# Three tiles in place of four in the row-wise opening of the gate projection of a transformer kernel

## The reference, cut to what matters

```python
for layer in range(DEPTH_2):
    ...
    h = h + rmsnorm(mix, gains[1])
    hn = rmsnorm(h, gains[2])
    ff = jnp.square(jax.nn.relu(hn @ w_up[layer])) @ w_down[layer]
    h = h + rmsnorm(ff, gains[3])
    gate = jax.nn.sigmoid(h @ w_ple_gate[layer])
    h = h + gate * (p[layer] @ w_ple[layer])
```

## Time and the profile before

| | us |
|---|---|
| median of 3 runs | 3325.06 (3324.88 to 3325.9) |
| the profiled execution, its own time | 3324.88 |
| its span | 3323.1 |
| PE busy | 3203.2 (96%) |
| POOL busy | 1743.3 (52%) |
| ACT busy | 1230.6 (37%) |
| DVE busy | 1214.4 (37%) |

### The profile page before, as it was taken

The page is one execution under the profiler, slowest core; times in us unless marked ns, Lnnn a source line. Parts: engine busy times, 40 slices in busy tenths (PEclk is TensorE's granted clock), DMA queues, the critical chain, the costliest instruction groups (busy, mean ns, idle before and its releaser), DMA issues.

```text
span 3323.1 us, 40114 instructions
## 1 busy us (share of the span) xinstructions
PE 3203.2 (96%) x15078; PEld 2612.8 (79%) x15078; DVE 1214.4 (37%) x2152; ACT 1230.6 (37%) x2217; POOL 1743.3 (52%) x1347
## 2 busy tenths in 40 slices
PE   8999999999999999999999898999999988999999
PEld 7888887777777787788888787877888776778887
DVE  4222322124555434223224655524111457341115
ACT  4332333333444435333224323234333345543333
POOL 6555655455554464465556213246555652475555
PEclk9999999999999999999999999999999999999999
DMA  4333222222222233333333102112333321223332
GB/s 163 98 92 101 86 86 76 83 82 77 64 61 61 70 106 97 88 98 98 98 96 95 54 26 58 39 54 80 101 96 95 96 70 39 64 85 100 96 101 86
DMA packets 149839, 275.58 MB, mean 83 GB/s; under 512 B 16528, under 2 KB 17808, under 8 KB 149520
## 3 DMA queue, kind: packets, MB, share of 16 engines
q1 hardware_dynamic: 149648, 273.02, 28.2%
HBM read 270.86 MB, written 2.10 MB: 82 GB/s over the span
## 4 chain that ended last, share of the span: by engine, by line
PE 85%; DVE 9%; POOL 3%; ACT 2%; issue 2%; DMA 0%; DVEq 0%; SPq 0%; ACTq 0%; POOLq 0%
PE PS L481 83%; PE PS L548 2%; POOL SM L2180 1%; DVE AR L1070 1%; POOL WL L2180 1%; DVE TMP L1070 1%; DVE ACC L1076 1%; DVE X L1070 1%; DVE AL L1070 1%; DVE HL L1076 1%; ACT AR L1795 1%; DVE SM L1070 1%; DVE TMP L1076 1%; DVE SM L1755 1%; DVE AR L1076 1%
## 5 line engine op out<-in xcount | busy, mean ns | idle before, releaser
L2180 POOL TENSOR_TENSOR WL<-RAW,WH 128x512 fp32r<-128x512 f32 x1002 | 1305.2, 1314 | 995.0 <-ACT WH L1795 994.2
L1795 ACT ACTIVATE WH<-RAW 128x512 fp32r<-128x512 f32 x1002 | 619.1, 627 | 1068.6 <-PE PS L481 1015.7
L481 PE MATMUL PS<-HH,WH 128*128 128x512 f32 x2296 | 914.0, 398 | 10.4 <-ACT WH L1795 7.1
L481 PE MATMUL PS<-HL,WH 128*128 128x512 f32 x2296 | 902.3, 393 | 7.9 <-DVE HL L1076 6.3
L481 PE MATMUL PS<-HH,WL 128*128 128x512 f32 x2296 | 901.5, 393 | 2.3 <-POOL WL L2180 2.3
L481 PE MATMUL PS<-AH,WH 128*128 128x512 f32 (+1 forms) x1504 | 584.3, 388 | 5.1 <-ACT AH L1795 3.5
L481 PE MATMUL PS<-AL,WH 128*128 128x512 f32 (+1 forms) x1504 | 582.1, 387 | 1.7 <-DVE AL L1070 1.1
L481 PE MATMUL PS<-AH,WL 128*128 128x512 f32 (+1 forms) x1504 | 580.9, 386 | 2.0 <-POOL WL L2180 2.0
L481 PEld LDWEIGHTS PS<-HL,WH 128*128 128x128 f32 x2296 | 435.7, 190 | 104.0 <-DVE HL L1076 12.1
L481 PEld LDWEIGHTS PS<-HH,WH 128*128 128x128 f32 x2296 | 435.3, 190 | 103.9 <-ACT WH L1795 7.4
L481 PEld LDWEIGHTS PS<-HH,WL 128*128 128x128 f32 x2296 | 434.8, 189 | 95.9 <-POOL WL L2180 4.2
(11 more groups left out here) (208 smaller groups left out, 2576.0 us busy)
## 6 DMA issues: line engine op xcount, KB each, us to landing
RAW<-in_wst SPq DMA_DIRECT2D x1002, 256.0 KB, 2.6
X<-in_x SPq DMA_DIRECT2D x8, 256.0 KB, 5.0
TMP<-in_p SPq DMA_DIRECT2D x8, 256.0 KB, 3.2
out<-X SPq DMA_DIRECT2D x8, 256.0 KB, 2.0
AR<-in_dm SPq DMA_DIRECT2D x1, 1024.0 KB, 5.3
AR<-in_mem SPq DMA_DIRECT2D x1, 1024.0 KB, 5.8
CST<-in_cst SPq DMA_DIRECT2D x1, 964.0 KB, 7.6
AR<-in_pos SPq DMA_DIRECT2D x2, 256.0 KB, 2.9
```

The costliest lines, as they stand in the source:

```text
L481: return e.matmul(o, l, r, start=a, stop=z, skip_group_check=True)
L1795: return e.activation(o, a, f, **kw)
L2180: return e.tensor_tensor(o, a, b, op)
```

## The change

The dictionary `opened`, which held the open PSUM banks by the kind of step, becomes two plain variables, `open_banks` and `mem_sum`, at all of its uses. In `e_open` the rows cover three output tiles in place of four; tile 3 is made by `lin` in step `e` of m = 3, and the waits of ScalarE follow.

```diff
-            opened = {}
+            open_banks = []
...
                 elif kind == "e_open":
                     l, k = i
                     if k == 0:
-                        opened[kind] = [bank("ple_gate", l, m) for m in range(4)]
-                    row_of(opened[kind], k, k == 0, k == 7, [("w_ple_gate_2", l, cc(128 * m)) for m in range(4)], "A",
-                           (("gate_hi", l, k), ("gate_lo", l, k)), ("e", l, 3) if k == 7 else None)
+                        open_banks = [bank("ple_gate", l, m) for m in range(3)]
+                    row_of(open_banks, k, k == 0, k == 7, [("w_ple_gate_2", l, cc(128 * m)) for m in range(3)], "A",
+                           (("gate_hi", l, k), ("gate_lo", l, k)), ("e", l, 2) if k == 7 else None)
                 elif kind == "e":
                     l, m = i
-                    if m > 3:
+                    if m > 2:
                         lin(("e", l, m), ("ple_gate", l, m), "w_ple_gate_2", l, cc(128 * m), range(8), "A")
...
                 elif kind == "e":
                     l, m = i
-                    e.wait_ge(*at("mm", "e", l, max(m, 3)))
+                    e.wait_ge(*at("mm", "e", l, max(m, 2)))
```

More of the change, by code:

```diff
@@ L578, in tensor @@
                     if k == 0:
-                        opened[kind] = [bank(w, f, m) for m in (0, 1) for w in ("gate", "up")]
+                        open_banks = [bank(w, f, m) for m in (0, 1) for w in ("gate", "up")]
                     tiles = [(w[f], 0, cc(128 * m)) for m in (0, 1) for w in (WG, WU)]
-                    row_of(opened[kind], k, k == 0, k == 7, tiles, "H", (("hi", n, k), ("lo", n, k)), ("f_open", f) if k == 7 else None)
+                    row_of(open_banks, k, k == 0, k == 7, tiles, "H", (("hi", n, k), ("lo", n, k)), ("f_open", f) if k == 7 else None)
                 elif kind == "f_extra":
@@ L599, in tensor @@
                     if k == 0:
-                        opened[kind] = [bank("r_even", 0, 0), bank("r_odd", 0, 0), bank("r_even", 0, 1)]
+                        open_banks = [bank("r_even", 0, 0), bank("r_odd", 0, 0), bank("r_even", 0, 1)]
                     tiles = [("w_in", 0, [(O_RQ, 2, 128)]), ("w_in", 0, [(O_RQ + 1, 2, 128)]), ("w_in", 0, [(O_RK, 2, 128)])]
-                    row_of(opened[kind], k, k == 0, k == 7, tiles, "H", (("hi", "nmix", k), ("lo", "nmix", k)), ("r_lin", 0, 2) if k == 7 else None)
+                    row_of(open_banks, k, k == 0, k == 7, tiles, "H", (("hi", "nmix", k), ("lo", "nmix", k)), ("r_lin", 0, 2) if k == 7 else None)
                 elif kind == "r_lin":
@@ L609, in tensor @@
                     if k == 0:
-                        opened[kind] = [bank("r_v", h, t) for t in range(4)]
-                    tok_row(opened[kind], k, "w_in", 0, O_RV + 512 * h, 512, "H", k == 0, k == 7, ("r_v", h) if k == 7 else None)
+                        open_banks = [bank("r_v", h, t) for t in range(4)]
+                    tok_row(open_banks, k, "w_in", 0, O_RV + 512 * h, 512, "H", k == 0, k == 7, ("r_v", h) if k == 7 else None)
                 elif kind == "r_sc":
@@ L710, in tensor @@
                         if m == 2:
-                            opened["nqm"] = bank("var", "nqm")
+                            mem_sum = bank("var", "nqm")
                         p = m // 2 - 1
                         e.wait_ge(*at("mq_pair", p))
-                        columns(opened["nqm"], p, tmp(2 + 2 * (p % 2)), one1, p == 0).then_inc(*up("mm", "mq_sum", p))
+                        columns(mem_sum, p, tmp(2 + 2 * (p % 2)), one1, p == 0).then_inc(*up("mm", "mq_sum", p))
                 elif kind == "nqm":
                     e.wait_ge(*at("mq_pair", 3))
-                    columns(opened["nqm"], 3, tmp(4), one1, False).then_inc(*up("mm", "mq_sum", 3))
+                    columns(mem_sum, 3, tmp(4), one1, False).then_inc(*up("mm", "mq_sum", 3))
                 elif kind == "mg":
@@ L731, in tensor @@
                         if m == 2:
-                            opened["nkm"] = bank("var", "nkm")
+                            mem_sum = bank("var", "nkm")
                         p = m // 2 - 1
                         e.wait_ge(*at("mk_pair", p))
-                        columns(opened["nkm"], p, tmp(2 + 2 * (p % 2)), one1, p == 0, 2).then_inc(*up("mm", "mk_sum", p))
+                        columns(mem_sum, p, tmp(2 + 2 * (p % 2)), one1, p == 0, 2).then_inc(*up("mm", "mk_sum", p))
                 elif kind == "nkm":
                     e.wait_ge(*at("mk_pair", 3))
-                    columns(opened["nkm"], 3, tmp(4), one1, False, 2).then_inc(*up("mm", "mk_sum", 3))
+                    columns(mem_sum, 3, tmp(4), one1, False, 2).then_inc(*up("mm", "mk_sum", 3))
                 elif kind == "mqn":
@@ L745, in tensor @@
                     if k == 0:
-                        opened[kind] = [bank("mv", g, t) for t in range(2)]
-                    tok_row(opened[kind], k, "mem_w_kv", 0, 1024 + 512 * g, 512, "A", k == 0, k == 7, ("mv", g) if k == 7 else None)
+                        open_banks = [bank("mv", g, t) for t in range(2)]
+                    tok_row(open_banks, k, "mem_w_kv", 0, 1024 + 512 * g, 512, "A", k == 0, k == 7, ("mv", g) if k == 7 else None)
                 elif kind == "ms":
@@ L779, in tensor @@
                     if k == 0:
-                        opened[kind] = [bank("conv_in", 0, j) for j in range(3)]
+                        open_banks = [bank("conv_in", 0, j) for j in range(3)]
                     tiles = [("w_in_ab_2", 0, cc(512 * j)) for j in range(3)]
-                    row_of(opened[kind], k, k == 0, k == 7, tiles, "H", (("hi", "na", k), ("lo", "na", k)), ("c", 0, 2) if k == 7 else None)
+                    row_of(open_banks, k, k == 0, k == 7, tiles, "H", (("hi", "na", k), ("lo", "na", k)), ("c", 0, 2) if k == 7 else None)
                 elif kind == "ab_gl":
@@ L960, in tensor @@
                     if k == 0:
-                        opened[kind] = [bank("mix_out", n, m) for m in range(3)]
+                        open_banks = [bank("mix_out", n, m) for m in range(3)]
                     need = (("ab_hi", k), ("ab_lo", k)) if n == "nab" else (("swa_hi", k), ("swa_lo", k))
-                    row_of(opened[kind], k, k == 0, k == ks[-1], [(name, 0, cc(128 * m)) for m in range(3)], "A", need,
+                    row_of(open_banks, k, k == 0, k == ks[-1], [(name, 0, cc(128 * m)) for m in range(3)], "A", need,
                            ("to", n, 2) if k == ks[-1] else None, None if n == "nab" else SWA_ROWS)
@@ L978, in tensor @@
                     if k == 0:
-                        opened[kind] = [bank("relu", l, m) for m in range(4)]
-                    row_of(opened[kind], k, k == 0, k == 7, [("w_up_2", l, cc(128 * m)) for m in range(4)], "H",
+                        open_banks = [bank("relu", l, m) for m in range(4)]
+                    row_of(open_banks, k, k == 0, k == 7, [("w_up_2", l, cc(128 * m)) for m in range(4)], "H",
                            (("hi", n, k), ("lo", n, k)), ("u", l, 3) if k == 7 else None)
@@ L1007, in tensor @@
                     if k == 0:
-                        opened[kind] = [bank("sq", u) for u in (8, 9, 0)]
-                    row_of(opened[kind], k, k == 0, k == 7, [("w_qkv_c_2", 0, SWA_COLS[u]) for u in (8, 9, 0)], "H",
+                        open_banks = [bank("sq", u) for u in (8, 9, 0)]
+                    row_of(open_banks, k, k == 0, k == 7, [("w_qkv_c_2", 0, SWA_COLS[u]) for u in (8, 9, 0)], "H",
                            (("hi", "nc1", k), ("lo", "nc1", k)), ("sl", 0) if k == 7 else None)
@@ L1016, in tensor @@
                     if k == 0:
-                        opened[kind] = [bank("sv", t) for t in range(4)]
-                    tok_row(opened[kind], k, "w_qkv_c_2", 0, 1280, 256, "H", k == 0, k == 7, ("sv",) if k == 7 else None)
+                        open_banks = [bank("sv", t) for t in range(4)]
+                    tok_row(open_banks, k, "w_qkv_c_2", 0, 1280, 256, "H", k == 0, k == 7, ("sv",) if k == 7 else None)
                 elif kind == "sr":
```

## The result

The changed kernel takes 3344.71 us, median of 4 runs (3339.94 to 3348.95), against 3325.48 for the kernel before (4 runs, 3324.88 to 3329.89). The ratio is 1.0054, 95% interval 1.0037 to 1.0072: slower, as forecast, but by 0.37 to 0.72% where 0.36% was forecast, and the time is outside the range of 3331 to 3341 us. Later, with the two run in turn on one chip, it was 3347.0 against 3330.22 us, ratio 1.0044 (1.0031 to 1.0056), 10 to 19 us.

What follows compares the result with a forecast made beforehand. TensorE bounds most of the kernel, with a cross-engine loop setting the row pace and the gate chain behind it in layer 0; 3324.88 plus 4.38 (layer 0) and 7.69 (layer 1) gave 3337 us, range 3331 to 3341.

Steps and rivals of the forecast that it cites:

- The loop of the rows: Gate projection rows, both layers: conversion, WL, AL and matmul follow one another without overlap; P1 to P7 takes 21.05 us.
- P steps: Gate projection rows: times between starts of the first matmuls with AL(k), from row 1 to row 7.
- list of signs: What the changed trace should show; for AL ending 0.55 us behind a WL it named rows 2, 3, 6, 7.
- The heavy gate step: Layer 0's gates: gate 3 also brings two panels, so a step of 4.03 becomes 6.25 us, +2.22.
- The sum: Both layers' gate projections together: 4.38 us for layer 0 plus 7.69 for layer 1, 12.1 us slower.
- rival 4: TensorE's clock falls in the new rows: at most 1.6 us a layer, or 7.8 throughout; 14%, nearly all the single fall.
- the wait ahead of 2677.97: Layer 0's gate steps: TensorE waits for WL without the slow clock returning, cited against the clock falling.
- the base: Whole kernel: the profiled execution's 3324.88 us, to which 12.07 us was added.
- Rival 1: Rows: only the moved matmuls count, the loop stays at 3.08 us; 5.0 us more, 3329.9 us; 13%.
- Rival 2: Rows: not slower, since AL escapes the fewer GpSimd subtractions and TensorE's 2.06 us decides; 3319.6 us; 5%.
- Rival 3: Layer 0 hides its cost if the chain of gates catches up, adding nothing; 3332.6 us; 8%.

Runs made afterwards that it cites:

- early AH: The changed kernel with ScalarE making AH(k+1) ahead of that row's panel conversion instead of behind it; 3331.53 against 3329.77 us, ratio 1.0010.
- padding: The changed kernel with one unused block behind the three of each row, so every row begins with a panel; 3333.43 against 3329.77 us, ratio 1.0006.
- fillers: The changed kernel with 18 extra matmuls a layer, results unused, in TensorE's gaps in the rows; 3345.08 against 3329.41 us, ratio 1.0045.
- layer 1 only: The kernel before with three tiles per row in layer 1, four kept in layer 0; 3337.66 us, ratio 1.0020.
- early AH with four tiles: The kernel before, four tiles in both layers, with AH(k+1) made ahead of the panel conversion; 3329.24 us, ratio 1.0002.
- shifted four: The kernel before with AH(k+1) made early and unused blocks so panels begin at each row's second tile; 3328.92 against 3329.41 us, ratio 0.9999.

## Why the prediction was right in its sum and wrong in its time

**The loop of the rows: right.** Forecast P steps 3.65, 4.34, 2.18, 2.89, 3.65, 4.34. Measured in layer 1 of the first profile, between starts of TensorE's matmuls with AL: 3.65 (3289.39 to 3293.04), 4.34, 5.07 for the two steps to 3302.45 together (2.18 + 2.89 = 5.07), 3.66, 4.36. AL of rows 2, 3, 5, 6 and 7 ended 0.54 to 0.56 us behind a WL; the prediction's own worked steps say so of row 5 too, though its list of signs leaves it out. That the order on ScalarE closes it was shown by early AH (21 to 13.8 us), that the panel's place does by padding (to 16.4).

**The heavy gate step: right.** Sigmoids 36.53 us apart, 36.5 forecast; 36.53 to 36.57 in all nine profiles with three tiles in layer 0, whatever the rows ahead did.

**The sum: right for a clock that stays up.** 4.38 + 7.69 forecast, 4.44 + 7.68 measured with fillers.

**The step that failed, in the mechanism: rival 4 and the evidence against it.** The prediction gave a fall of the clock 14% and put it into the sum at nothing, since the clock stood at 1.00 through the rows of the kernel before. But those rows have TensorE nearly full (2.93 of 3.00 us), while its own working left TensorE idle for over a third of the new ones (2.06 us of matmuls in a mean row of 3.51). The fall came in ten of ten such stages, 1.3 to 1.6 us for one and 2.7 to 2.8 for two: some +3 us. Its size for a single fall, at most 1.6 us, was right, its chance wrong. The other piece of evidence, that the wait ahead of 2677.97 brought no fall, holds for one profile only. In the second profile of the same kernel the same wait of 1.44 us is followed by a fall:

```profile
2683.27 0.51 PE L481 MATMUL PS<-AH,WL 128*128 128x512 f32 x1 [1.44 <-POOL WL L2180]
...
2684.39 0.63 PE L481 MATMUL PS<-AH,WH 128*128 128x512 f32 x1
```

Three more of the five profiles with four tiles in layer 0 have it there (layer 1 only, early AH with four tiles, shifted four). It cost nothing, 58.37 against 58.48 us, since the chain of gates sets the pace in these steps. So one trace without a fall was weak evidence.

The Trainium skill ("TensorE: Matmul & The Clock Gate", "HAM oscillation") tells of a tile loop in which waits of about 3 to 5 us bring the slow clock back every time. The waits in these rows are shorter, up to 0.9 us each, ahead of a row's first matmul and behind it, and a fall came once or twice in a stage of eight rows; rows at half speed throughout (+7.8 us a layer) were never seen.

**The step that failed, in the time: the base, too low and too narrow.** With a single fall in each layer the prediction itself gets 3340.2 us, inside its range, so the clock in the rows alone doesn't carry the time out. Of the 7.8 us between 3336.95 and 3344.71 some 3 are those falls, and the rest, nearly 5, is the base. The absolute time was built on one execution of 3324.88 us, within 1 us of the three known. Twenty-nine later runs of the same kernel have a median of 3330.22 us and reach 3337.64: the median is 5.3 us above that execution. 3330.2 + 12.1 + 3 is 3345.3 us, against medians of 3344.71 and 3347.0. The difference of 12.1 + 3 us is 0.45% of the time, as the later ratio has it (1.0044); the first one, 1.0054, was taken against a base of four runs of which three lay at the low end. The stretch between adds 0.6 to 4.8 us in the four profiles of the changed kernel. That it adds something on average because of the change isn't shown.

**The rivals.** Rival 1 (moved matmuls only) fell by the loop itself, though padding nearly made it true (+2.7 us in the stages for 5.0 worked out). Rival 2 needed AL to escape WL; in the changed kernel it doesn't in five of the six rows, it does in the padded, early-AH and shifted kernels, where WL holds X in its place, and no kernel here is shown faster than the one before. Rival 3 fell: layer 0 cost its share in every profile.

## What to carry to other kernels

When work is cut into rows and weights into panels, ask where in a row the panel begins: a panel that begins behind the wait for the row's operand chains TensorE, ScalarE, GpSimd and VectorE one behind the other, and taking work out of the row makes it longer. An in-order engine should make what the next row waits for ahead of a refill that is needed five panels later. Where a change opens gaps on TensorE, put a fall of its clock into the sum, and don't take one trace without a fall as evidence against it. Take the base from more than a few runs before quoting a range of a few us.

## What the runs showed of the hardware

One kernel, unchanged, spread over 12.7 us (3324.91 to 3337.64) in 29 runs on one chip, and 5.4 us of difference between two of its profiles had built up ahead of 2642 us, with 10.2 us more at 1.2 GHz. A DVE operation with two SBUF inputs that met a running GpSimd subtraction ended 0.54 to 0.56 us after it, and one with a PSUM and an SBUF input was not held (0.74 us while WL ran, padded kernel). The Trainium skill ("SBUF — State Buffer", "SBUF: two separate sides") calls the pair of ports that VectorE and GpSimd share an exclusive lock that goes to whoever starts first; the rows agree, X or AL being held by the rest of WL and not slowed in proportion, but for the end: AL alone takes 0.68 us and here ends 0.54 behind WL, 0.14 sooner than waiting for all of WL would give. Eighteen matmuls a layer whose results nobody uses kept the clock up and shortened the two stages by 1.3 and 1.6 us against the first profile of the changed kernel; the whole is not shown faster by it.
